# An expert's down weights in one load of 4 MB in place of two of 2 MB, in a hybrid block with 32 experts

## What is computed

```python
def expert_block(args):
    xb, e = args
    return (jax.nn.silu(xb @ w_gate[e]) * (xb @ w_up[e])) @ w_down[e]
```

## Time and profile before

| what | value |
|---|---|
| runs | 1670.22, 1671.82, 1673.20 us; median 1671.82 |
| the profiled execution's own time | 1668.66 us |
| its span | 1666.9 us |
| PE busy | 1553.7 us, 93% |
| DMA queue q1 (SP's loads) | 470.84 MB, 69.8% of 16 engines over the span |
| down loads | 63 of 2 MB, median 15.8 us from issue to landing |

### The profile page before, as it was taken

One profiled execution on the slowest core, in us unless ns is written; L12 is line 12 of the kernel. 1 busy time (PEld: TensorE's weight loads), 2 busy tenths in 40 slices (PEclk: granted clock), 3 DMA queues, 4 the chain that ended last, 5 costly groups with the idle time before them and its releaser, 6 DMA issues.

```text
span 1666.9 us, 18187 instructions
## 1 busy us (share of the span) xinstructions
PE 1553.7 (93%) x7236; PEld 894.2 (54%) x7236; DVE 637.7 (38%) x774; ACT 357.5 (21%) x639; POOL 165.2 (10%) x235
## 2 busy tenths in 40 slices
PE   7999999999999999799999899889889899899998
PEld 7788777768887567634343433434434334343343
DVE  6656656652223433513233322322323323323224
ACT  6422333352222244211110110011011011101011
POOL 4470044510000000100000000000000000000000
PEclk9999999999999999999999999999999999999999
DMA  8332322353215031799999999999999999999997
GB/s 304 102 101 79 94 61 70 103 183 101 96 56 202 1 127 44 320 377 429 412 424 429 428 428 429 428 423 420 429 417 417 428 420 428 428 426 428 424 421 290
DMA packets 90237, 484.47 MB, mean 291 GB/s; under 512 B 6066, under 2 KB 44108, under 8 KB 62156
## 3 DMA queue, kind: packets, MB, share of 16 engines
q1 hardware_dynamic: 86696, 470.84, 69.8%
q0 software_dynamic: 3392, 12.92, 2.3%
q10 hardware_dynamic: 100, 0.03, 0.0%
HBM read 484.81 MB, written 8.39 MB: 296 GB/s over the span
## 4 chain that ended last, share of the span: by engine, by line
PE 68%; DMA 17%; DVE 8%; ACT 3%; issue 2%; SPq 1%; POOL 0%; DVEq 0%; POOLq 0%; ACTq 0%
PE ps L2232 23%; DMA weight_ring<-in_expert_w_up_dram 15%; PE ps L1939 10%; PE ps L1813 8%; PE ps L2258 8%; PE ps L2193 5%; PE ps L1992 3%; DVE residual L1618 3%; ACT weight_ring L887 1%; PE ps L1775 1%; DMA residual<-in_x_dram 1%; PE ps L2321 1%; PE ps L2056 1%; DVE weight_ring L1290 1%; PE ps L2081 1%
## 5 line engine op out<-in xcount | busy, mean ns | idle before, releaser
L2232 PE MATMUL ps<-weight_ring,transposed_acts 128*64 128x512 f32 x2000 | 467.6, 610 | 40.2 <-DMA weight_ring<-in_expert_w_up_dram 39.4
L2232 PEld LDWEIGHTS ps<-weight_ring,transposed_acts 128*64 128x64 f32 x2000 | 169.0, 140 | 331.6 <-issue 260.1
L1618 DVE TENSOR_TENSOR residual<-ps,residual 128x1024 f32<-128x1024 f32 x128 | 150.8, 1219 | 249.6 <-PE ps L2193 249.2
L2258 PE MATMUL ps<-weight_ring,transposed_acts 128*64 128x512 f32 x960 | 214.1, 599 | 17.8 <-DVE transposed_acts L1628 17.8
L1634 DVE SCALAR_TENSOR_TENSOR y_low<-ps,proj_buffer,y_high 64x1024 fp32r<-64x1024 f32 x60 | 77.0, 1283 | 199.4 <-ACT y_high L1079 198.4
L2258 PEld LDWEIGHTS ps<-weight_ring,transposed_acts 128*64 128x64 f32 x960 | 67.6, 138 | 146.8 <-issue 142.7
L1079 ACT ACTIVATE y_high<-ps,proj_buffer 64x1024 fp32r<-64x1024 f32 x60 | 66.5, 1109 | 288.1 <-PE ps L2258 287.3
L1813 PE MATMUL ps<-mix_high,w_in_high 128*128 128x512 f32 x288 | 117.8, 409 | 1.3 <-issue 1.3
L1068 ACT ACTIVATE transposed_acts<-ps 128x512 f32<-128x512 f32 x32 | 19.1, 598 | 464.7 <-PE ps L2232 464.7
L1813 PE MATMUL ps<-mix_high,w_in_low 128*128 128x512 f32 x288 | 112.8, 392 | 0.0
L1813 PE MATMUL ps<-normed_low,w_in_high 128*128 128x512 f32 x288 | 112.7, 391 | 0.0
(11 more groups left out here) (323 smaller groups left out, 1889.3 us busy)
## 6 DMA issues: line engine op xcount, KB each, us to landing
weight_ring<-in_expert_w_down_dram SPq DMA_DIRECT2D x63, 2048.0 KB, 15.8
weight_ring<-in_expert_w_gate_dram SPq DMA_DIRECT2D x61, 2048.0 KB, 16.3
weight_ring<-in_expert_w_up_dram SPq DMA_DIRECT2D x60, 2048.0 KB, 20.5
weight_ring<-in_w_in_dram SPq DMA_DIRECT2D x18, 1024.0 KB, 5.6
weight_ring<-in_w_out_dram SPq DMA_DIRECT2D x16, 1024.0 KB, 5.0
weight_ring<-in_xkv_w_dram SPq DMA_DIRECT2D x8, 1024.0 KB, 7.6
residual<-in_x_dram SPq DMA_DIRECT2D x8, 1024.0 KB, 12.8
weight_ring<-in_xq_w_dram SPq DMA_DIRECT2D x4, 1024.0 KB, 9.7
```

What stands on the lines that cost most here:

```text
L1618: v.tensor_tensor(part, ps[:, bank:bank + 2, :].rearrange("p b n -> p (b n)"), part, ALU.add).then_inc(signal, 1)
L2232: ins = mm(ps[side * SLOTS:(side + 1) * SLOTS, 0, :], xsT[:, k, par * SLOTS:(par + 1) * SLOTS], gate_up_weights(e, u, kk), start=(k == 0), ...
L2258: ins = mm(ps[half, 4 + n % 2, :], act_t[:, f * SLOTS:(f + 1) * SLOTS], w[:, n * 512:(n + 1) * 512], start=(f == 0), stop=(f == KF - 1), s ...
```

## The change

For every expert that `load_units` loads (1 to 29), unit 4's iteration is left out. In unit 5's, SP waits until PE has used unit 5, the later of the two, and then issues one DMA of 4 MB into slots 8 to 11, with one run of 32 KB for each partition. Its landing raises unit 4's semaphore (`landed[8]`). In `down`, PE waits for that semaphore ahead of the first half and for nothing ahead of the second; only expert 0, whose halves are still loaded apart, keeps both waits. The counts that PE waits for on unit 5's semaphore are now written out for the three experts that still use it (0, 30 and 31).

```diff
             def load_units(e, b, which):
                 for u in which:
+                    if u == 4:
+                        continue
                     sp.wait_ge(used, b * 6 + (UE - 6 + u + 1))
+                    if u == 5:
+                        sp.dma_start(ring[:, 8 * CHK:NSLOT * CHK], expert_w_down[0].rearrange("e (p f) n -> e p (f n)", f=KF)[
+                            ds(e, 1)].rearrange("e p m -> p (e m)")).then_inc(landed[unit_slot(4)], 16)
+                        continue
                     sp.dma_start(unit(u), expert_unit(e, u)).then_inc(landed[unit_slot(u)], 16)
...
+                elif u == 5:
+                    pe.wait_ge(landed[s], 16 * (early_loads[s] + {0: 1, NE - 2: 2, NE - 1: 3}[b]))
...
-                    if f % 2 == 0:
+                    if f == 0 or f == 2 and isinstance(b, int) and b == 0:
                         expert_landed(e, u)
```

## The result

The changed kernel takes 1672.91 us (median of 20 runs, 1668.83 to 1678.43) against 1669.60 for the kernel before (20 runs beside them, 1665.88 to 1673.20). The ratio is 1.0022, with an interval of 1.0015 to 1.0029: slower by 3.7 us, 2.5 to 4.8. The forecast was +1.7.

What follows compares the result with a forecast made beforehand. The prediction took the DMA engines' weight loading to bound the expert stage. Its terms, +3.4 us at expert 1 and -1.7 for longer runs, put on the median of 1671.82, gave 1673.5 us (+1.7), range 1669.0 to 1677.5.

Steps and rivals of the forecast that it cites:

- What bounds the kernel: Expert stage: weights come as fast as the DMA engines move them; only time per byte and engine idle time count.
- The later issue at expert 1: Expert 1's down load meets an empty queue, so engines idle 3.43 us longer and nothing gives it back: +3.4 us.
- Cost in all experts but the first: nothing: Steady pairs of blocks: the 4 MB load, though issued later, is ready before the queue empties; no cost.
- The cover of 1.4 us: Odd block at 1024 us: the 4 MB load is ready 1.4 us before the queue would be empty.
- The rival of the empty queue: SP's later down loads: queue runs empty in odd blocks too, 9.6 us there, 1685 us in all; chance 0.12.
- the prediction's own sign of being wrong: Block 7 to block 29: prediction wrong if this stretch changes by more than 4 us, either way.
- The longer runs, -1.7 us: Down loads: 32 KB runs in place of 16 KB save 64 ns an expert, 1.7 us for 27 experts.
- the bounds of 0.9 and 2.6: Gain of the down loads' 32 KB runs, in us, at 4 ns and 12 ns that don't grow with the run.
- One DMA in place of two, nothing: Down loads: start and completion of the second lie beside the moving of the first; leaving one out gains nothing.
- The sum: Whole kernel: + 3.4 - 1.7, that is +1.7 us, giving 1673.5 us.
- "within 0.2%": Whole kernel: a time within 0.2% of the kernel before, which measurement can't tell from no change; chance 0.71.

Runs made afterwards that it cites:

- The kernel with expert 1 alone: Against the kernel before, only expert 1's down weights come in one load of 4 MB, experts 2 to 29 as before; ratio 1.0027, +4.5 us.
- the odd kernels: Against the kernel before, only odd experts 3 to 29 load later: one 4 MB load, or two of 2 MB behind the later wait; 1.0017 each, +2.8 us.

## Why the prediction was right or wrong

*What bounds the kernel:* right. In the steady part the DMA share stays near 1 (0.99 with the change), and in the main the stretch grows by what the engines lose at the down loads (table).

*The later issue at expert 1, +3.4 us:* right in place and size. The idle stretch lasts past 738 us, unit 3 of expert 2 lands 3.4 us later against PE's block 1, and PE waits 2.4 us for it. The kernel with expert 1 alone gives +4.5 (2.7 to 6.3).

*"Cost in all experts but the first: nothing":* this is the step that failed. The cover of 1.4 us was worked out from a landing, and a load has landed when the last of 16 engines is through. The others are through earlier, and for them there was no cover. The rival of the empty queue had the place, but tied it to the wrong condition: it asked for more than 3.6 us beside the moving. Where the odd experts' load met an empty queue it was 2.1 us, and the loss came all the same. Its price of 9.6 us in the odd experts was too high for the usual run: the odd kernels show 2.8 to 3.7 us in 14 experts, 0.20 to 0.26 us each. In the profiled execution, the longest, it was 7.7 us in eleven. There the prediction's own sign of being wrong came true: the stretch that was not to change by more than 4 us grew by 5.6.

*The longer runs, -1.7 us:* right. The runs are whole (4,176 packets fewer), and 0.08 us an expert, some 2 us in 27, lies between the bounds of 0.9 and 2.6. In a run's time it stays below what the intervals can tell.

*One DMA in place of two, nothing:* right within what can be told, since the packets' 0.07 us leave 0.01 of the 0.08. The Trainium skill (page "DMA: Bandwidth & Descriptors", section "Anatomy of one DMA") gives a fixed cost of about 2.0 us, for DMAs that GpSimd issues. The traces have near it, 2.1 and 2.2 us beside the moving, for two of SyncE's loads into a queue that is empty or nearly so, and 3.6 for the 4 MB at expert 1. But 29 such shares did not come back: in a full queue they lie beside the moving.

*The sum:* 3.4 - 1.7 and, in the odd experts, about 2.8 to 3.7 that I had at nothing, makes 4.5 to 5.4; measured 3.7 (2.5 to 4.8). The terms and the whole agree within their intervals; so, only just, do the two halves of the change measured apart, +4.5 for expert 1 and +1.7 for the others, 6.2 together. The time lay in the range, and the sign was right. That is in part luck, as the term that I had at nothing came out at 0 to 7.7 us in the profiled executions of kernels that have the later issue behind the same queue. And the forecast "within 0.2%" is not what the interval of 1.0015 to 1.0029 supports best.

What stays open: how the early engines' idle time becomes a loss of the last one. With nearly the same time from issue to unit 3's landing (3.48 to 3.49 us) three odd experts of the changed kernel lost 0.0, 0.3 and 1.2 us. The share above 1 at the start (1.27, and 1.69 at expert 1) says that packets that begin together behind an empty queue take longer than they do in a full one; whether the last engines are slowed by that, or change places with others, no view here tells by engine, and no run separates it.

## What to carry to other kernels

Where transfers are the bound, a larger transfer that has to wait for the later of two buffers trades a few ns for each longer run against the moment of issue; look at what is in the queue at that moment, load by load, and at the first of the stage above all, where the queue is shortest. The landing of the load ahead is the last engine's, so a cover counted to it promises too much; counted to the moment when the first engines run out it is on the safe side. If the cover is short, other work of the releasing engine can be moved into a place where it waits anyway; here that took the loss out of the landings.

## What was not expected of the hardware

A run that starts behind an empty queue takes longer for its bytes. The first 16 runs of 32 KB at expert 1 took 1.47 to 2.10 us each by the trace's packets, those of the even experts of the steady part, behind a full queue, mostly 1.21 to 1.22. In the odd expert shown, the 2 us in which most engines start have a share of 1.27 at 418 GB/s, against 1.04 at 442 in the 2 us before. And the changed kernel's 20 runs spread over 9.6 us, the 20 of the kernel before over 7.3; that the near-empty queue makes the difference is likely, not shown.
